# Strassen's seven products for two token chunks of a down-projection, with sums formed by accumulating DMAs

## The chip, the cores and the metric

One core of a Trainium2 chip runs one inference step of a one-layer hybrid decoder in float32. The metric is the device time of one execution in microseconds (us). The kernel uses TensorE (PE, matmuls; PEld its weight loads), VectorE (DVE), ScalarE (ACT), GpSimd (POOL) and SyncE (SP, which issues most DMAs).

## The reference, cut to what matters

The layer is an FFN, then attention and gated delta branches, then a second FFN (FFN 2). Only FFN 2 is touched.

```python
def swiglu(x, w_in, w_out):
    gate, up = jnp.split(x @ w_in, 2, axis=-1)
    return (jax.nn.silu(gate) * up) @ w_out
...
    y = h + 0.5 * rmsnorm(swiglu(rmsnorm(h, p['ffn2_pre']), p['ffn2_w_in'], p['ffn2_w_out']), p['ffn2_post'])
```

There are 1056 tokens (1024 of the prompt and 32 sampled), the model width is 1024, and D_FF is 2816, which is 22 tiles of 128. The down-projection is a 1056 x 2816 by 2816 x 1024 product.

## The kernel before

Each engine has its program written out by hand and waits on semaphores; nothing else orders the work. `ffn_units` builds both FFNs, `outputs_ffn` what surrounds FFN 2. Float32 products are made of two rounded halves: ScalarE casts a value to its high part, VectorE subtracts to get the low part, and TensorE does three matmuls (high by high, high by low, low by high).

*Gate stage.* Two of the 22 tiles of D_FF are computed plainly. For each of the other twenty (loop over t, line 2740) `product` does seven Strassen products of 24 matmuls with 264 columns. GpSimd makes four sums of the weight tiles in `s_buf` (lines 2829 to 2834), VectorE combines the products and multiplies gate by up in `pair_h`, and `store_h` writes the tile to `d_hid` in DRAM, in two halves of the tokens. SP loads the pair of weight tiles two ahead (`load_pair`).

*Down-projection.* Tokens are in three chunks: 384, 384 and 288 (`SPANS`). The loop over h goes through six passes: h // 2 is the chunk, h % 2 the half of 512 output columns. A pass has 22 steps k, one for each tile of D_FF, and each step has 4 output blocks x 3 matmuls (`out_step`, line 2897). A pass sums in four PSUM banks, the next one in the other four. The weight tile of step u is loaded by `load_unit` into one of eight 256 KB slots, cast by `unit_high` (2568) and split by `unit_low` (2572), three steps before TensorE uses it, into one of four slots. So a cast waits until TensorE has finished with the step four before it. The hidden tiles come back from `d_hid` through four staging buffers (`load_hid`), are cast (2594) and split (2600) into `hid_hi` and `hid_lo`, and serve both halves. The first ten are prepared within the last tile of the gate stage:

```python
    EARLY = {2: range(0, 3), 3: range(3, 6), 4: range(6, 8), 5: range(8, 10)}
```

*After a chunk.* `square` (ScalarE) and `copy_out` (VectorE) empty PSUM into `acc`; `sum_pool` (GpSimd, 2981), `sum_y` (PE, 2989) and `root_y` (ScalarE, 3001 and 3003, each with a table load) give the norm; `norm` (3010) and `resid` (3981) on VectorE scale and add the residual, which `res_load` brings; then TensorE transposes (`turn`, 4120) and ScalarE copies rows out (3849). These are placed into steps of the next passes by functions named `during(h, k)` for each engine. `turn_residual` (4141) and `res_row` (3853) do the same for the residual of chunk 2, whose own norm is applied at the very end.

## Time and profile before

| what | value |
|---|---|
| time, median of 3 runs | 3401.08 us (3397.26 to 3401.41) |
| span of the profiled execution | 3400.1 us |
| TensorE busy | 3305.8 us, 97% |
| VectorE, ScalarE, GpSimd busy | 1871.2, 1456.3, 700.0 us |
| DMA | 390.03 MB, mean 115 GB/s |

The profiled execution has no time of its own beside these; its span runs from its first to its last instruction. Busy times of matmuls overlap, because they are pipelined, so the rate of TensorE is read from starts or from long pieces, not from the mean duration.

### The profile page before, as it was taken

Reading aid. Unit: us, or ns where it says so; the run is one execution under the profiler, and the core shown is the slowest. Engines: PE = TensorE matmul, PEld = TensorE weight load, DVE = VectorE, ACT = ScalarE, POOL = GpSimd, SP = SyncE. Lnnn points to the kernel's source line nnn. Section 1 sums busy time; section 2 is a strip of 40 time slices with the busy share of each in tenths; the row PEclk is TensorE's granted clock in tenths of the full one; section 3 lists DMA queues with packets and bytes.
Section 4 is the critical chain, followed back from the end, with each engine's and each line's share of the span. In section 5 each row is a group of like instructions: output and inputs, shape, how many; then the busy total and the mean of one; then the engine's idle time right before and its main releaser. Section 6 shows DMA issues by size and latency. Waiting matters only on the chain. (4 is left out here: it accounts for less than half of the span.)

```text
span 3400.1 us, 70872 instructions
## 1 busy us (share of the span) xinstructions
PE 3305.8 (97%) x28190; PEld 3137.6 (92%) x28190; DVE 1871.2 (55%) x3334; ACT 1456.3 (43%) x3056; POOL 700.0 (21%) x651
## 2 busy tenths in 40 slices
PE   7999999998999999999999999999999899999999
PEld 7999999997888888877899999998999899999998
DVE  6655565764555555554455555554441855556555
ACT  5222234555555455443344444444323722223444
POOL 3323310112222222100022222222001332221000
PEclk9999999999999999999999999999999999999999
DMA  4222237742222222379511122224532322224664
GB/s 167 76 79 79 87 109 230 221 135 81 70 70 70 71 70 70 109 254 369 188 47 56 58 59 59 59 59 136 165 88 70 123 86 76 76 76 151 200 207 132
DMA packets 353606, 390.03 MB, mean 115 GB/s; under 512 B 22792, under 2 KB 259416, under 8 KB 353134
## 3 DMA queue, kind: packets, MB, share of 16 engines
q1 hardware_dynamic: 343126, 352.18, 33.1%
q0 software_dynamic: 10080, 33.05, 2.7%
q8 instruction: 228, 3.74, 0.5%
q14 instruction: 88, 0.72, 0.1%
q10 hardware_dynamic: 84, 0.35, 0.0%
HBM read 309.92 MB, written 75.57 MB: 113 GB/s over the span
## 5 line engine op out<-in xcount | busy, mean ns | idle before, releaser
L673 PE MATMUL ps<-p_hi,w_hi 128*128 128x352 f32 x912 | 305.6, 335 | 1.8 <-PEq L123 1.4
L673 PE MATMUL ps<-p_hi,w_lo 128*128 128x352 f32 x912 | 294.5, 323 | 0.0
L673 PE MATMUL ps<-p_lo,w_hi 128*128 128x352 f32 x912 | 294.0, 322 | 0.0
L2062 PE MATMUL ps<-p_hi,w_hi 128*128 128x352 f32 x840 | 291.0, 346 | 2.7 <-PEq L123 1.4
L2062 PE MATMUL ps<-p_hi,w_lo 128*128 128x352 f32 x840 | 277.2, 330 | 0.0
L2062 PE MATMUL ps<-p_lo,w_hi 128*128 128x352 f32 x840 | 277.2, 330 | 0.0
L673 PEld LDWEIGHTS ps<-p_hi,w_hi 128*128 128x128 f32 x912 | 173.1, 190 | 4.2 <-issue 2.7
L2897 PE MATMUL ps<-op_hid_hi,w_hi 128*128 128x384 f32 (+1 forms) x528 | 171.5, 325 | 3.7 <-DVE w_lo L2572 2.0
L673 PEld LDWEIGHTS ps<-p_lo,w_hi 128*128 128x128 f32 x912 | 173.2, 190 | 0.0
L2897 PE MATMUL ps<-f_hid_hi,w_hi 128*128 128x352 f32 x528 | 171.5, 325 | 1.6 <-DVE w_lo L2572 1.6
L673 PEld LDWEIGHTS ps<-p_hi,w_lo 128*128 128x128 f32 x912 | 172.2, 189 | 0.0
L2897 PE MATMUL ps<-f_hid_lo,w_hi 128*128 128x352 f32 x528 | 170.0, 322 | 0.0
L2897 PE MATMUL ps<-f_hid_hi,w_lo 128*128 128x352 f32 x528 | 169.9, 322 | 0.0
L2897 PE MATMUL ps<-op_hid_hi,w_lo 128*128 128x384 f32 (+1 forms) x528 | 169.6, 321 | 0.0
L2897 PE MATMUL ps<-op_hid_lo,w_hi 128*128 128x384 f32 (+1 forms) x528 | 169.6, 321 | 0.0
L2062 PEld LDWEIGHTS ps<-p_hi,w_hi 128*128 128x128 f32 x840 | 160.5, 191 | 8.2 <-issue 3.1
L2062 PEld LDWEIGHTS ps<-p_lo,w_hi 128*128 128x128 f32 x840 | 160.9, 192 | 0.2
L2062 PEld LDWEIGHTS ps<-p_hi,w_lo 128*128 128x128 f32 x840 | 160.5, 191 | 0.0
L2572 DVE TENSOR_TENSOR w_lo<-w_raw,w_hi 128x512 fp32r<-128x512 f32 x136 | 100.5, 746 | 83.2 <-ACT w_hi L2568 82.8
L414 ACT ACTIVATE at_prob<-ps,at_nmax 128x256 f32<-128x256 f32 (+7 forms) x128 | 94.2, 737 | 82.4 <-DVE at_nmax L520 80.7
L2568 ACT CAST w_hi<-w_raw 128x512 fp32r<-128x512 f32 x136 | 83.8, 620 | 100.5 <-PE ps L2897 100.1
L347 ACT ACTIVATE at_rotx<-ps 32x352 f32<-32x352 f32 x192 | 87.4, 455 | 88.6 <-DVE at_cosx L468 54.7
(707 smaller groups left out, 10374.4 us busy)
## 6 DMA issues: line engine op xcount, KB each, us to landing
w_raw<-in_ffn_w_out_dram SPq DMA_DIRECT2D x136, 256.0 KB, 3.4
w_raw<-in_w_in_dram SPq DMA_DIRECT2D x67, 512.0 KB, 4.2
sa_v<-in_cache_v_dram SPq DMA_DIRECT2D x120, 256.0 KB, 6.7
w_raw<-in_ffn_w_in_dram SPq DMA_DIRECT2D x48, 512.0 KB, 5.1
sa_k<-in_cache_k_dram SPq DMA_DIRECT2D x72, 256.0 KB, 5.5
f_s<-in_ffn_w_out_dram SPq DMA_DIRECT2D x64, 256.0 KB, 3.5
pair_s<-in_ffn_w_out_dram SPq DMA_DIRECT2D x64, 256.0 KB, 3.2
d_hid<-f_gb SPq DMA_DIRECT2D x44, 264.0 KB, 2.1
```

The lines of the kernel that those rows point to most:

```text
L347: ins = nc.scalar.mul(dst, src, HD ** -0.5 if kind == "q" else 1.0)
L414: nc.scalar.activation(pr[:, i % 2, a, 0:(i + 1) * P], m.ps[:, 2 + 2 * a:4 + 2 * a, :].rearrange("p b k -> p (b k)")[:, 0:(i + 1) * P], AC ...
L673: mm = nc.tensor.matmul(m.ps[:, bank, 0:CH], a[:, k, w], b[:, f, cols(c)], start=(f == 0 and i == 0), stop=(f == KT - 1 and i == 2))
L2062: mm = nc.tensor.matmul(m.ps[:, (k + c) % 2, 0:CH], a[:, k, f * P:(f + 1) * P], x[:, f, cols(c)], start=(j == 0), stop=(j == len(terms) - 1))
L2568: nc.scalar.copy(unit_slot(u, False), unit_raw(u)).then_inc(e.out_hi, 1)
L2572: nc.vector.tensor_tensor(unit_slot(u, True), unit_raw(u), unit_slot(u, False).bitcast(F32), ALU.subtract).then_inc(e.out_lo, 1)
L2897: mm = nc.tensor.matmul(m.ps[:, bank, 0:hi - lo], unit_slot(u, low_part)[:, o * P:(o + 1) * P], y[:, k, 0:hi - lo], start=(k == 0 and n == ...
```

## The change

Chunks 0 and 1 (768 tokens) are multiplied by Strassen's scheme. The 22 tiles of D_FF are split into two times 11 (KH), the output columns into two halves, the tokens into the two chunks. Seven products p of 11 steps each take the place of four passes of 22 steps. Chunk 2 keeps its two passes, now h = 7 and 8.

- *Weights.* Product 0 and 5 use a block of `w_out` as it is. The sums for products 1, 2 and 3 (33 tiles) are formed in DRAM during the gate stage: SP copies one tile to `d_w` (`copy_pairs`), GpSimd issues a DMA that adds the other (`add_pairs`). Products 4 and 6 load two tiles for each step and VectorE subtracts them (`w_sum`), 22 times.
- *Hidden tiles.* Tiles 11 to 21 are stored negated (`pair_h`), so that sums become differences. SP writes the first chunk of tiles 0 to 10 twice more (`store_sums`), and GpSimd's accumulating DMAs form the operands of products 0, 4, 5 and 6 in DRAM (`add_stored`, `add_lower`). VectorE forms that of product 3 (`x_sum`). Each operand is cast and split in three groups of 4, 4 and 3 tiles (`x_high`, `x_low`), each a single instruction.
- *Results.* A product's four banks are read in two pieces of 2 x 384. ScalarE writes blocks of `acc` first (`read_act`), VectorE adds to or subtracts from them (`read_dve`). `acc` now holds both chunks.
- *Order.* The work after chunk 0 goes into products 5 and 6, with the transposes of its rows at steps 7 to 9 of product 6; the work after chunk 1 goes into h = 7. The norm of chunk 1 is at step 9 of h = 7, where it had been at step 6 of h = 4; residual rows are still at steps 8, 10, 12. The cast of chunk 2's hidden tiles runs from product 6 into h = 7, and GpSimd makes their low parts (`rest_low`), in between its sums of squares.

```diff
+    KH = FT // 2
+    W3 = 3 * P
+    WL = T - 2 * W3
+    GROUPS = ((0, 4), (4, 8), (8, KH))
+    SOURCES = (((1, 1),), None, None, None, ((1, 0), (1, 1)), ((0, 0),), ((0, 1), (0, 0)))
...
+    COPIES = [(p, k) for p in PAIRED for k in range(KH)]
+    READ_ACT = (4, 6, 8, 8, 8, 8, 8)
...
+    def copy_pairs(sp, t):
+        for p, k in COPIES[2 * (t - 2):2 * (t - 1)]:
+            a, half = PAIRED[p][0]
+            sp.dma_start(d_w[p - 1, k], wout[:, k + KH * a, half * 512:half * 512 + 512]).then_inc(e.w_copied[t % 2], 16)
+    def add_pairs(pool, t):
+        if 2 * (t - 2) < len(COPIES):
+            pool.wait_ge(e.w_copied[t % 2], 16 * (2 * ((t - 2) // 2) + len(COPIES[2 * (t - 2):2 * (t - 1)])))
+        for p, k in COPIES[2 * (t - 2):2 * (t - 1)]:
+            a, half = PAIRED[p][1]
+            pool.dma_start(d_w[p - 1, k], wout[:, k + KH * a, half * 512:half * 512 + 512], accum_op=ALU.add).then_inc(e.w_added, 16)
...
+    def store_sums(sp, t):
+        for d in (d_first, d_sum):
+            sp.dma_start(d[t], hid[:, 0:W3]).then_inc(e.x_out, 16)
+    def add_stored(pool, s):
+        j = s - KH
+        if s < KH:
+            for a in range(2):
+                pool.wait_ge(e.h_out[a], 16 * (s + 1))
+            pool.wait_ge(e.x_out, 32 * (s + 1))
+            wait(pool, e.added[6], 16 * s)
+            pool.dma_start(d_sum[s], hid_part(s, 1), accum_op=ALU.add).then_inc(e.added[6], 16)
+            return
+        pool.wait_ge(e.h_out[0], 16 * (s + 1))
+        if j == 0:
+            pool.wait_ge(e.x_out, 32 * KH)
+            pool.wait_ge(e.added[6], 16 * KH)
+        wait(pool, e.added[0], 16 * j)
+        pool.dma_start(d_first[j], hid_part(s, 0), accum_op=ALU.add).then_inc(e.added[0], 16)
+        pool.wait_ge(e.h_out[1], 16 * (s + 1))
+        pool.dma_start(hid_part(j, 1), hid_part(s, 1), accum_op=ALU.add).then_inc(e.added[5], 16)
+    def add_lower(pool, s):
+        pool.wait_ge(e.added[0], 16 * (s - KH + 1))
+        pool.dma_start(hid_part(s, 0), hid_part(s, 1), accum_op=ALU.add).then_inc(e.added[4], 16)
+    def load_first_parts(sp, g):
+        lo, hi = GROUPS[g]
+        if g < 2:
+            sp.wait_ge(e.up_mm, 12 + N1 - 6)
+        else:
+            sp.wait_ge(e.up_mm, 12 + N1)
+        sp.wait_ge(e.added[0], 16 * hi)
+        sp.dma_start(FIRST[g], d_first[lo:hi].rearrange("k p n -> p k n")).then_inc(e.first_in[g], 16)
+    def load_quad(sp, p, k):
...
+        src = {1: (k, 0), 2: (KH + k, 1), 4: (KH + k, 0), 5: (k, 1)}
+        sp.dma_start(HOME[p][:, k, :], d_sum[k] if p == 6 else hid_part(*src[p])).then_inc(e.quad_in[p], 16)
...
+    def x_high(act, p, g):
...
+            act.wait_ge(e.up_mm, 12 + N1 - 7 + (2, 3, 4, 6)[(GROUPS[g][1] * W3 - 1) // (HALF * HT)])
+        elif p >= 2:
+            act.wait_ge(e.out_mm, KH * (p - 1))
+        nc.scalar.copy(x_slot(hid_hi, p, g), x_value(p, g)).then_inc(e.hid_hi, 1)
...
+    def w_sum(dve, v):
+        r = RAW_OF[v]
+        raw_there(dve, r)
+        raw_there(dve, r + 1)
+        nc.vector.tensor_tensor(unit_raw(r), unit_raw(r), unit_raw(r + 1), ALU.subtract).then_inc(e.w_sum, 1)
...
+    def w_high(act, v):
+        if v in SUM_OF:
+            act.wait_ge(e.w_sum, SUM_OF[v])
+        else:
+            raw_there(act, RAW_OF[v])
...
+            act.wait_ge(e.up_mm, 12 + N1 - 10 + v + 1)
...
+        if lower_rest(v):
+            nc.scalar.mul(unit_slot(v, False), unit_raw(RAW_OF[v]), -1.0).then_inc(e.out_hi, 1)
+        else:
+            nc.scalar.copy(unit_slot(v, False), unit_raw(RAW_OF[v])).then_inc(e.out_hi, 1)
...
+    def rest_high(act, n):
+        act.wait_ge(e.hid_full[n % 4], 16 * (n // 4 + 1))
+        act.wait_ge(e.out_mm, KH * 6 if n < 14 else KH * 7)
+        nc.scalar.copy(rest_tile(hid_hi, n), staged(2, n % 4)[:, 0:WL]).then_inc(e.rest_hi, 1)
+    def rest_low(pool, n):
+        pool.wait_ge(e.rest_hi, n + 1)
+        nc.gpsimd.tensor_tensor(rest_tile(hid_lo, n), staged(2, n % 4)[:, 0:WL], rest_tile(hid_hi, n).bitcast(F32), ALU.subtract).then_inc(e.rest_lo, 1)
...
+    def read_act(act, q):
+        if q in (0, 1, 2):
+            act.wait_ge(e.out_mm, KH * (q + 1))
...
+            for i in (1, 0):
+                for half in range(2):
+                    nc.scalar.mul(block_of(i, 0, half), pass_bank(q, half), -1.0).then_inc(e.read_act, 1)
...
+            for half in range(2):
+                nc.scalar.mul(block_of(1, 1, half), pass_bank(q, half), -1.0).then_inc(e.read_act, 1)
+        elif q == 2:
...
+    def add_block(q, i, j, sign=1.0):
+        for half in range(2):
+            y = block_of(i, j, half)
+            if q in (1, 2):
+                nc.vector.wait_ge(e.read_act, READ_ACT[q - 1] + half + 1)
+            if sign > 0:
+                nc.vector.tensor_tensor(y, pass_bank(q, half), y, ALU.add).then_inc(e.read_dve, 1)
+            else:
+                nc.vector.scalar_tensor_tensor(out=y, in0=pass_bank(q, half), scalar=-1.0, in1=y, op0=ALU.mult, op1=ALU.add).then_inc(e.read_dve, 1)
+    def read_dve(dve, q, second):
+        if not second:
+            dve.wait_ge(e.out_mm, KH * (q + 1))
+            wait(dve, e.read_dve, READ_DVE[q - 1])
+        if q == 1:
+            if not second:
+                add_block(q, 1, 0)
+        elif q == 2:
+            if not second:
+                add_block(q, 0, 0)
+        elif q == 3:
+            add_block(q, *((1, 1) if second else (0, 0)))
+        elif q == 4:
+            if not second:
+                add_block(q, 0, 0, -1.0)
+        elif q == 5:
+            add_block(q, *((1, 1) if second else (0, 1)))
+        elif not second:
+            add_block(q, 1, 1)
...
+            copy_pairs(sp, t)
+            store_h(sp, t, 0)
+            if t < KH:
+                store_sums(sp, t)
+            store_h(sp, t, 1)
+        for g in range(2):
+            load_first_parts(sp, g)
+        for r in range(4, 8):
+            load_raw(sp, r)
+        store_h(sp, FT - 1, 0)
+        store_h(sp, FT - 1, 1)
+        r = 8
+        def raws(v):
...
+        for v in range(NQ):
+            p, k = divmod(v, KH)
+            raws(v + 6 if p else v + 8)
+            if v == 0:
+                for n in range(4):
+                    load_quad(sp, 1, n)
+            elif v == 1:
+                for n in range(4, 8):
+                    load_quad(sp, 1, n)
+            elif v == 2:
+                for n in range(8, KH):
+                    load_quad(sp, 1, n)
+            elif v == 3:
+                load_first_parts(sp, 2)
+            elif 5 <= v <= 15:
+                load_quad(sp, 2, v - 5)
+            elif 22 <= v <= 32:
+                load_quad(sp, 4, v - 22)
+            elif 33 <= v <= 43:
+                load_quad(sp, 5, v - 33)
+            elif 44 <= v <= 54:
+                load_quad(sp, 6, v - 44)
+            elif v == 62:
+                for n in range(4):
+                    load_rest(sp, n)
+            elif p == 6 and k >= 3:
+                load_rest(sp, k + 1)
+            during(p, k)
+        for h in range(2):
+            for k in range(FT):
+                raws(NQ + h * FT + k + 6)
+                if h == 0 and 12 + k < FT:
+                    load_rest(sp, 12 + k)
+                during(7 + h, k)
+    def quad_scalar(act, during):
+        for v in range(NQ):
+            p, k = divmod(v, KH)
+            w_high(act, v + 3)
+            if p == 0:
+                if k == 5:
+                    x_high(act, 0, 2)
+                elif k in (7, 9):
+                    x_high(act, 1, (k - 7) // 2)
+            else:
+                if k == 0:
+                    read_act(act, p - 1)
+                elif p == 1 and k in (2, 5, 7, 9):
+                    x_high(act, 1 if k == 2 else 2, {2: 2, 5: 0, 7: 1, 9: 2}[k])
+                elif k in (2, 4, 6) and 1 < p < 6:
+                    x_high(act, p + 1, k // 2 - 1)
+                elif p == 6 and k >= 2:
+                    rest_high(act, k - 2)
+            during(p, k)
+        for h in range(2):
+            for k in range(FT):
+                v = NQ + h * FT + k
+                if v + 3 < NQ + 2 * FT:
+                    w_high(act, v + 3)
+                if h == 0 and 9 + k < FT:
+                    rest_high(act, 9 + k)
...
+    def quad_vector(dve, during):
+        for v in range(NQ):
+            p, k = divmod(v, KH)
+            w_low(dve, v + 3)
+            if v + 4 in SUM_OF:
+                w_sum(dve, v + 4)
+            if p == 0:
+                if k == 6:
+                    x_low(dve, 0, 2)
+                elif k in (8, 10):
+                    x_low(dve, 1, k // 2 - 4)
+            elif p == 1:
+                if k in (3, 6, 8, 10):
+                    x_low(dve, 1 if k == 3 else 2, {3: 2, 6: 0, 8: 1, 10: 2}[k])
+            else:
+                if k == 0:
+                    read_dve(dve, p - 1, False)
+                elif k == 1 and p == 2:
+                    x_sum(dve, 0)
+                elif k == 2:
+                    if p == 2:
+                        x_sum(dve, 1)
+                    read_dve(dve, p - 1, True)
+                elif k in (3, 5, 7) and p < 6:
+                    x_low(dve, p + 1, (k - 3) // 2)
+                elif k == 4 and p == 2:
+                    x_sum(dve, 2)
+            during(p, k)
+        for h in range(2):
+            for k in range(FT):
+                v = NQ + h * FT + k
...
+    def quad_gpsimd(pool, during):
+        for n in range(8):
+            rest_low(pool, n)
+        sum_pool(pool, 1, 1, 4)
+        for n in range(8, 11):
+            rest_low(pool, n)
+        sum_pool(pool, 1, 4, 6)
+        for n in range(11, 13):
+            rest_low(pool, n)
+        sum_pool(pool, 1, 6, 8)
+        for n in range(13, FT):
+            rest_low(pool, n)
+    def quad_tensor(pe, during, bank_free):
+        for p in range(7):
+            for k in range(KH):
+                v = KH * p + k
+                during(p, k)
+                pe.wait_ge(e.out_lo, v + 1)
+                for g in range(3):
+                    if k == GROUPS[g][0]:
+                        pe.wait_ge(e.hid_lo, part_count(p, g))
...
+                    for n, (low_part, y) in enumerate(((False, hid_hi), (False, hid_lo), (True, hid_hi))):
+                        mm = nc.tensor.matmul(m.ps[:, 4 * (p % 2) + o, 0:W3], unit_slot(v, low_part)[:, o * P:(o + 1) * P], y[:, x, :],
+                                              start=(k == 0 and n == 0), stop=(k == KH - 1 and n == 2))
+                mm.then_inc(e.out_mm, 1)
...
         dve.wait_ge(e.up_done, 6 + 2 * (t - 2) + 2 - a)
-        nc.vector.tensor_tensor(hid[:, halves(a)], hid[:, halves(a)], silu[:, halves(a)], ALU.mult).then_inc(e.h_done, 1)
+        if not quads or t < KH:
+            nc.vector.tensor_tensor(hid[:, halves(a)], hid[:, halves(a)], silu[:, halves(a)], ALU.mult).then_inc(e.h_done, 1)
+            return
+        nc.vector.scalar_tensor_tensor(out=hid[:, halves(a)], in0=hid[:, halves(a)], scalar=-1.0, in1=silu[:, halves(a)],
+                                       op0=ALU.mult, op1=ALU.mult).then_inc(e.h_done, 1)
 
     def vector(dve, scale_in, between, during):
...
+            if quads:
+                if t > 2:
+                    add_pairs(pool, t - 1)
+                if t > 2 + KH:
+                    add_lower(pool, t - 3)
+                add_stored(pool, t - 2)
+        if quads:
+            add_lower(pool, FT - 3)
+            add_stored(pool, FT - 2)
+            add_lower(pool, FT - 2)
+            add_stored(pool, FT - 1)
+            add_lower(pool, FT - 1)
+            during()
+            quad_gpsimd(pool, during)
 
...
+                nc.scalar.copy(row_of(6 + t).rearrange("p (b f) -> p b f", b=2), m.ps[:, 2:4, :]).then_inc(res_moved, 1)
 
             def during(h, k):
-                if h == 4 and k in (8, 10, 12):
+                if h == 3 and k in (7, 8, 9, 10):
+                    e.square(act, k - 7)
+                elif h == 5 and k in (1, 2):
+                    e.square(act, 2 + 2 * k)
+                    e.square(act, 3 + 2 * k)
+                elif h == 5 and k == 7:
+                    e.root_y(act, 0, 3)
+                elif h == 6 and k in (5, 6):
+                    e.square(act, 2 * k - 2)
+                    e.square(act, 2 * k - 1)
+                elif h == 6 and k in (7, 8, 9):
+                    row(k - 7)
+                elif h == 7 and k in (1, 2):
+                    e.square(act, 10 + 2 * k)
+                    e.square(act, 11 + 2 * k)
+                elif h == 7 and k in (8, 10, 12):
                     res_row((k - 8) // 2)
-                if h in (2, 4):
...
-                c = h // 2 - 1
-                if h in (2, 4):
-                    if 8 <= k < 12:
-                        e.norm(dve, c, 2 * (k - 8), 5 * KT)
-                        e.norm(dve, c, 2 * (k - 8) + 1, 5 * KT)
-                    elif k in (12, 13):
-                        resid(c, k - 12)
+                pairs = {(5, 9): (0, 0), (5, 10): (0, 1), (6, 1): (0, 2), (6, 3): (0, 3), (7, 10): (1, 0), (7, 11): (1, 1), (7, 12): (1, 2), (7, 13): (1, 3)}
+                sums_of = {(6, 4): (0, 0), (6, 5): (0, 1), (7, 14): (1, 0), (7, 15): (1, 1)}
+                if (h, k) in pairs:
...
 
             def during(h, k):
-                if h == 4 and k in (7, 9, 11):
+                if h == 5 and k == 6:
+                    pe.wait_ge(e.read_dve, e.READ_DVE[4])
+                    e.sum_y(pe, 0, 3)
+                if h == 6 and k in (7, 8, 9):
+                    turn(k - 7)
+                if h == 7 and k in (7, 9, 11):
                     turn_residual((k - 7) // 2)
-                if h == 4 and k == 17:
-                    pe.wait_ge(res_moved, 3)
-                if h == 5 and k == 10:
-                    pe.wait_ge(e.y_copied, 2 * KT + HALF)
+                if h == 7 and k == 8:
+                    e.sum_y(pe, 1, 0)
+                if h == 7 and k in (17, 18, 20):
+                    turn({17: 3, 18: 4, 20: 5}[k])
```

## Rows read from the trace of the kernel before

**Rows 1.** The page: span, busy times, the granted clock in 40 slices.
```profile
span 3400.1 us, 70872 instructions
...
PE 3305.8 (97%) x28190; PEld 3137.6 (92%) x28190; DVE 1871.2 (55%) x3334; ACT 1456.3 (43%) x3056; POOL 700.0 (21%) x651
...
PEclk9999999999999999999999999999999999999999
```

**Rows 2.** The chain that ended last, from 2700 us: start, length, what.
```profile
2709.02 392.84 PE ps L2887 x3216
...
3127.28 95.97 PE ps L2897 x552
...
3330.82 9.48 PE ps L2897 x72
```

**Rows 3.** Who waited for whom, 3113 to 3401: us in total, times, longest.
```profile
PE ps L2897 <- DVE w_lo L2572: 2.0, 2, 1.7
...
PE ps L2897 <- ACT plain L3849: 1.7, 2, 1.0
...
PE ps L4141 <- ACT plain L3853: 0.8, 1, 0.8
```

**Rows 4.** Windows: busy us by engine (instructions), clock, DMA share, GB/s.
```profile
core 0: us, PE busy (x) PEld busy (x) DVE busy (x) ACT busy (x) POOL busy (x), PEclk, DMA share, GB/s
2900.00:3000.00 100.00, 100.00 (x825) 100.00 (x824) 57.12 (x89) 27.26 (x48) 31.25 (x20) 1.00 0.28 81
3180.00:3190.00 10.00, 10.00 (x60) 10.00 (x59) 5.82 (x10) 4.93 (x10) 0.00 (x0) 1.00 1.03 361
3190.00:3200.00 10.00, 10.00 (x59) 10.00 (x58) 5.74 (x11) 5.17 (x10) 0.00 (x0) 1.00 0.85 252
```

**Rows 5.** A group of the gate stage: VectorE reading PSUM; busy, mean ns, idle.
```profile
L2774 DVE TENSOR_TENSOR op_gb<-ps,pair_tmp 128x528 f32<-128x528 f32 x19 | 13.4, 707 | 28.2 <-PE ps L2887 28.2
```

**Rows 6.** Groups of GpSimd, 500 to 1600 us: DMAs that it issues.
```profile
L615 POOL DMA_DIRECT2D d_gates<-at_gate x15 | 8.3, 556 | 28.5 <-ACT at_gate L358 28.5
L600 POOL DMA_DIRECT2D out_k_prompt_dram<-at_k_rows x8 | 7.9, 992 | 289.2 <-ACT at_k_rows L375 245.2 <-issue 44.0
```

**Rows 7.** DMA issues (KB, us to landing), and SP's waits, gate stage.
```profile
d_hid<-op_gb SPq DMA_DIRECT2D x38, 264.0 KB, 2.2
...
pair_s<-in_ffn_w_out_dram SPq DMA_DIRECT2D x64, 256.0 KB, 3.2
...
SPq L2510 <- DVE op_gb L2723: 331.8, 36, 14.8
```

**Rows 8.** The start of the down-projection: VectorE's timeline; TensorE's line 2897.
```profile
3125.91 0.71 DVE L2723 TENSOR_TENSOR op_gb<-op_gb 128x528 f32<-128x528 f32 x1 [0.71 <-ACT op_gb L2673]
3126.54 0.68 DVE L2572 TENSOR_TENSOR w_lo<-w_raw,w_hi 128x512 fp32r<-128x512 f32 x1
...
L2897 PE MATMUL ps<-op_hid_hi,w_hi x528: 289/334/631, 3119.1 to 3388.8; 128*128 128x384 f32 x118, 128*128 128x288 f32 x58
```

**Rows 9.** Groups of instructions by shape, 3113 to 3401 us.
```profile
L2572 DVE TENSOR_TENSOR w_lo<-w_raw,w_hi 128x512 fp32r<-128x512 f32 x68 | 49.1, 728 | 49.8 <-ACT w_hi L2568 49.4
...
L2568 ACT CAST w_hi<-w_raw 128x512 fp32r<-128x512 f32 x68 | 42.0, 621 | 58.8 <-PE ps L2897 58.6
...
L2600 DVE TENSOR_TENSOR op_hid_lo<-plain,op_hid_hi 128x384 fp32r<-128x384 f32 x44 | 24.9, 572 | 9.7 <-ACT op_hid_hi L2594 9.5
...
L2981 POOL TENSOR_TENSOR op_gb<-op_gb 128x384 f32<-128x384 f32 x14 | 16.4, 1171 | 210.1 <-ACT op_gb L2966 208.7
...
L2594 ACT CAST op_hid_hi<-plain 128x288 fp32r<-128x288 f32 x22 | 9.5, 431 | 5.2 <-DMA plain<-d_hid 5.1
L3010 DVE SCALAR_TENSOR_TENSOR acc_chunk<-acc_chunk,gain,op_gb 128x384 f32<-128x384 f32 x16 | 9.1, 612 | 0.0
...
L3981 DVE TENSOR_TENSOR acc_chunk<-acc_chunk,plain 128x1536 f32<-128x1536 f32 x4 | 7.0, 1752 | 0.0
...
L3853 ACT COPY plain<-ps 128x1024 f32<-128x1024 f32 x3 | 3.0, 1006 | 0.0
...
L3001 ACT ACT_TABLE_LOAD x2 | 2.6, 1283 | 0.0
```

373 lines of the change are left out of this document (307 added, 66 removed).

## The prediction

> **What bounds the kernel now.** I read the page first: TensorE is busy 3305.8 us of a span of 3400.1 us and its clock reads 9 in all forty slices [rows 1]. Next the chain that ended last, in order of time, for the stage that the change touches [rows 2]. From 2709.02 it is TensorE in one unbroken piece, the gate stage (3216 of its 3360 matmuls), and then the down-projection, again TensorE in long pieces. A kernel whose chain is one engine gets faster only by less work on it, or by fewer waits of it. The table of waits [rows 3] says how few there are in the down-projection: 2.0 us for VectorE's low parts and 1.7 us for ScalarE's row copies on PE's own rows, 0.8 for the residual transposes. So removed matmuls are worth their full price, and each microsecond by which another engine comes late is paid in full. The windows [rows 4] give the cover: while TensorE is full, VectorE is busy 57 of 100 us in the gate stage and 5.8 of 10 later, ScalarE 27 of 100 and 5 of 10. The DMA share is 0.28 in the gate stage, but 0.85 to 1.03 while hidden tiles and residual are loaded.
>
> **What is removed.** For token chunks 0 and 1 the product was 4 passes x 22 steps x 12 matmuls of 384 columns = 1056. Seven products x 11 steps x 12 are 924, so 132 go. Durations in the table overlap, so the price is the pitch: 552 matmuls in 95.97 us [rows 2] = 0.1739 us. That is -22.95 us. A step of 12 is 2.09 us, a product 23.0 us. Chunk 2 keeps its 528 matmuls of 288 columns (9.48 us for 72, 0.132 each; a step of 1.58 us). Transposes and sums on TensorE stay the same in number.
>
> **Gate stage.** Its matmuls don't change. One pair of tiles takes 168 matmuls x 392.84/3216 = 20.5 us. GpSimd is busy 31.25 of 100 us with its four sums [rows 4], 6.4 us of a pair, so 14.1 are free. It now issues accumulating DMAs in each pair: two weight sums and one hidden sum at first (pairs 3 to 12), five in pairs 14 to 18, four in 13 and 19. No accumulating DMA is in the trace. GpSimd's plain ones take 0.54 us (528 KB) to 0.99 us (512 KB) of its time [rows 6]: 2.7 to 5.0 us for five, hidden. Their waits are for stores that land 2.2 us after issue [rows 7] and were issued before GpSimd starts that pair, so nothing queues behind them for long; what is queued is the next pair's sums, which VectorE and ScalarE need about three products (9 us) before TensorE would starve. SP gains four plain DMAs in a pair (two 256 KB copies, two 192 KB); it waits 331.8 us of this stage for hidden tiles [rows 7], so their issue is covered. In bytes a pair has 1.5 MB at share 0.28; the change adds 0.9 MB of plain and up to 1.1 MB of accumulating transfers, each of which reads twice. Even at three times a plain one's price that is share 0.7. VectorE's 528-wide multiply gets a sign in 22 cases, beside idle time. I cost the stage at nothing; floor 0, ceiling under the rivals.
>
> **Start of the down-projection.** Before, VectorE's last gate product and the low part of step 3 come at 3125.9 to 3127.2 [rows 8], and TensorE, which begins at 3119.1, loses 1.7 us. After, ten hidden casts (5.5 us of VectorE, ten of 0.57) become two 1536-wide ones before step 3 (1.75 each, from the residual sum's row in [rows 9]), so VectorE is 2 us earlier and that wait goes. A new one comes at step 8: the third group of the first operand needs, from the last hidden half at about 3122, a store (2.2 us), an accumulate (I take 4 us: plain 256 KB ones land in 3.2), a load behind 2.2 MB of product 1's tiles and four weight tiles (3.2 MB at 361 GB/s, 9 us from 3124), its own 0.6 MB and a cast (1.2) and a low part (1.4). It is ready near 3139; step 8 is due at 3119.1 + 16.7 = 3135.8. +3.2, minus the 1.7: **+1.5 us** (0 to 7).
>
> **The seven products, VectorE.** Weights for step v+3 may be cast when step v-1 is done: 0.62 + 0.73 us, against 3 steps of 6.26, so VectorE may lag by 4.9 us before TensorE waits. Its operations, by [rows 9] where no other group is named: low part 0.73; weight sum 0.73; a 768-wide addition from PSUM 0.95 (0.707 for 528 in [rows 5], and 1.0 ns for each further element, the slope between the 512 and 1536 wide rows); low part of four tiles 1.75, of three 1.36; norm 0.61. Product 4: 11 low parts, 7 sums, 4 additions, 3 low parts of the next operand, 8.0 + 5.1 + 3.8 + 4.9 = 21.8 of 23.0 us, but front-loaded: steps 0 to 6 hold 17 us against 14.6. The lag, about 3, stays under 4.9. Products 1, 2, 3 and 5 hold less. Product 6: steps 0 to 5 hold 6 low parts, 6 sums, 4 additions, 4 norms and 2 residual sums = 4.4 + 4.4 + 3.8 + 2.4 + 3.5 = 18.5 us, after a start late by 1.7 (two norm pairs in product 5's last steps). At step 7, 14.6 us in, TensorE must transpose what the residual sums gave, ready at 20.2. **+5.4 us**, less 0.6 for the same wait of before. No row shows a queue as full as this, so 0 (transposes just in time) to 8.
>
> **DMA.** In product 4, and again in 6, a step needs two 256 KB weight tiles and one hidden tile of 192 KB (147 KB in 6): 721 kB in 2.09 us, 345 GB/s, against 220 before. [Rows 4] show 361 GB/s at share 1.03 and, ten microseconds later, 252 at 0.85, which is 296 at full share. By 361 nothing is lost; by 296 a step lasts 2.44 us, so 3.9 in each product, and the last residual's 1.18 MB in product 6 is 4.0 more: 11.8. The row nearest to this mix of tiles is the first, so **+1 us**. The Trainium skill (DMA: Bandwidth & Descriptors, Specifications) puts the HBM limit per core at about 358 GB/s; by that this term is 0 and the sum 1 us lower, and the 361 of the trace agrees.
>
> **Chunk 2's first half.** The norm of chunk 1 moves from step 6 to step 9, to between two residual-row copies. From step 8 ScalarE has a weight cast, a hidden cast (0.43) and a copy (1.0): 2.05; then step 9's casts and the root (two table loads of 1.28 and two passes of some 0.55), 1.05 + 3.7; then step 10's 2.05: 8.85 us. TensorE needs that second copy at step 11, 4.7 + 1.2 us in: 2.9 late. The norms and residual sums then end near 20.7, TensorE's step 17 comes at 19.1: 1.6. Together 4.5, against 1.8 in [rows 3]: **+2.7 us** (0 to 5). GpSimd's 22 low parts (0.9 each, three quarters of the 384-wide row) and seven sums of 1.17 [rows 9] are 28 us, over some 54: hidden.
>
> **Sum.** -22.95 + 1.5 + 5.4 - 0.6 + 1 + 2.7 = -12.95. The shown times are 3401.08 median (3397.26 to 3401.41); the profiled execution's span is 3400.1, so what lies around it is about 1.0 us and stays. 3401.1 - 13.0 = **3388 us**.
>
> **The rivals.**
> All new work is hidden: VectorE's rows are long enough and every wait above is an overestimate. Then only the matmuls count and the old 2.3 us go too: 3376. For it: 5 to 6 us of lag come from adding mean durations. Against: product 6's queue is full by count. 0.16.
> DMA binds products 4 and 6, and queued weight tiles arrive late: 296 GB/s instead of 361, and the accumulated lag cannot be won back, up to +11.8 - 1: 3395 to 3399. For it: the second window of [rows 4]. 0.22.
> GpSimd sets the pace of the gate stage, the case that ends slower. It decides from 14.1/5 = 2.8 us for an accumulating DMA. At 4 us each, a pair with five takes 6.4 + 20 = 26.4 instead of 20.5, five times, and one with four 22.4, twice: +33, so 3421. Against it: 0.54 to 0.99 in [rows 6]; for it: none of those computes. The Trainium skill (SBUF — State Buffer, Who interferes with whom) says that software descriptor generation is starved while VectorE is in a two-port mode, and that its tensor_tensor has none. By that rule this case stays away; no row here has a DMA of GpSimd's beside such a mode, so the trace doesn't settle it. The chance is 0.12.
> The forecast as summed, 3383 to 3393: 0.50.
>
> **How the numbers follow.** 0.2% (6.8 us) is about what a measurement of this kernel can tell from no change. Faster: the forecast's 0.50 less 0.02, the hidden case's 0.16, and a little of the DMA case, 0.03: 0.67. Same: most of the DMA case and the edge of the forecast: 0.21. Slower: 0.12. The range goes from 3375 (all hidden) to 3402 (both 296 GB/s and the upper ends of the start); it leaves out the GpSimd case and slivers.
>
> **What the changed profile would show.** 924 matmuls of 384 columns at a pitch of 0.174; the gate stage still one piece of 3216 or more at 0.122; GpSimd's accumulating DMAs under 1 us each in it, with its four sums starting every 20.5 us. One wait of TensorE for a low part of hidden tiles some 17 us into the down-projection; one of about 5 us at the transposes in product 6, whose releaser is VectorE's residual sum; two in chunk 2's first half, released by ScalarE's residual copy and VectorE's residual sum. DMA share near 1 in products 4 and 6. The prediction is wrong if the gate stage stretches, if weights arrive late in products 4 and 6 (VectorE's weight sums waiting for DMA), or if VectorE's reads of PSUM take much more than 0.95 us.

## The result: no gain, and 28 us of waits and half clock where 10 us of waits were forecast

The changed kernel took 3406.7 us in the median of 20 runs (3399.55 to 3413.99), the kernel before 3400.23 us beside it (20 runs, 3394.21 to 3405.44): ratio 1.0018, 95% interval 1.0012 to 1.0025. Forecast was 3388 (3375 to 3402). So it is slower by 0.18%, 6 us, and 19 us off the forecast.

The profiled execution is the longest of its 20 runs (3413.99 us). The page of the changed kernel, beside [rows 1]: 132 matmuls fewer, and nearly as much busy TensorE.
```profile
span 3412.4 us, 70726 instructions
...
PE 3297.4 (97%) x28058; PEld 3127.3 (92%) x28058; DVE 1892.9 (55%) x3303; ACT 1464.0 (43%) x3030; POOL 784.2 (23%) x750
...
PEclk9999999999999999999999999899999999999999
...
q0 software_dynamic: 21168, 50.35, 6.1%
```
The one 8 in the clock's row is slice 26 (2133 to 2218 us), in a stage that the change doesn't touch; slices of 85 us are too coarse for what follows. The chain that ended last (start, length, what), beside [rows 2]:
```profile
2714.32 410.27 PE ps L3408 x3360
...
3150.49 69.22 PE ps L3054 x384
```
The gate stage is one piece of 3360 matmuls, 0.1221 us each, the same pitch as before. It starts 5.3 us later than in [rows 2]: that much of the difference of the two traces was there before any touched line. From here on I compare the rest of the span, from the first matmul of the down-projection: 3400.1 - 3119.1 = 281.0 us before, 3412.4 - 3124.4 = 288.0 after, +7.0. This comparison leaves the jitter of earlier stages out and agrees with the 6 us of the medians. It is still one execution of each kernel. The part behind the last matmul of chunk 2 is 10.7 us before and 11.9 in the changed kernel, but 10.9 to 11.0 in ten of the twelve edited kernels below, none of which touches it: about 1 us of the 7.0 is chance of this execution, and "rest" makes each edit below look some 1 us better than it is.

Who waited for whom on TensorE from 3120 on (total, times, longest), beside [rows 3]:
```profile
PE ps L3054 <- DVE op_hid_lo L2761: 9.2, 1, 9.2
PE ps L4677 <- DVE acc_chunk L4537: 8.0, 2, 6.6
PE ps L4700 <- ACT plain L4397: 5.1, 2, 4.7
PE ps L3061 <- ACT plain L4393: 1.0, 1, 1.0
PE ps L3061 <- DVE w_lo L2798: 0.7, 1, 0.7
PE ps L3054 <- DVE w_lo L2798: 0.6, 2, 0.4
PE ps L3061 <- DVE w_lo L2795: 0.3, 1, 0.3
```
That is 24.9 us against 4.5. Three waits make 20.5 of it: at step 8 of product 0 (L3054), at chunk 0's transposes in product 6 (6.6 of L4677) and at a residual row block in chunk 2's first half (4.7 of L4700). The windows of these places, beside [rows 4], and of the gate stage (busy us by engine, clock, DMA share, GB/s):
```profile
2720.00:3120.00 400.00, 400.00 (x3293) 400.00 (x3292) 230.68 (x355) 111.94 (x195) 180.56 (x149) 1.00 0.64 154
3140.00:3160.00 20.00, 10.78 (x49) 10.49 (x48) 7.49 (x8) 7.24 (x10) 0.00 (x0) 0.74 0.88 300
3280.00:3300.00 20.00, 13.44 (x72) 13.12 (x71) 18.88 (x24) 8.55 (x18) 6.89 (x6) 0.81 0.79 257
3320.00:3340.00 20.00, 14.17 (x89) 13.21 (x89) 6.54 (x10) 13.00 (x22) 8.20 (x10) 0.83 0.93 319
```
The last column but two, the granted clock, is what I had no term for. It is 1.00 in the gate stage and 0.74 to 0.83 in the three windows with a long wait; of the other windows of 20 us up to 3380 only the one behind 3300 is below 1.00 (0.94). TensorE's timeline behind the first (start, length) shows what that means for work:
```profile
3150.49 0.66 PE L3054 MATMUL ps<-op_hid_hi,w_hi 128*128 128x384 f32 x1 [9.22 <-DVE op_hid_lo L2761]
3150.94 0.52 PE L3054 MATMUL ps<-op_hid_lo,w_hi 128*128 128x384 f32 x1
3151.26 0.52 PE L3054 MATMUL ps<-op_hid_hi,w_lo 128*128 128x384 f32 x1
...
3155.74 0.34 PE L3054 MATMUL ps<-op_hid_lo,w_hi 128*128 128x384 f32 x1
3155.91 0.34 PE L3054 MATMUL ps<-op_hid_hi,w_lo 128*128 128x384 f32 x1
```
Starts are 0.32 us apart until 3155.74 and 0.17 after it: the clock stood at its lower level of 1.2 GHz. These 5.25 us hold 16 matmuls, worth 2.8 us at 0.1739: 2.5 us lost. The length of this stretch is in part chance: behind the same wait (8.9 to 9.7 us) it is 2.8 us in e3, 3.0 in e7 and 5.5 in e10, so 1.4 to 2.8 us are lost. In product 6 the eight transposes and the step behind the 6.6 us wait take 5.6 us (3296.74 to 3302.34), where the next transposes take 0.9 and a step 2.1: 2.6 lost. Behind the 4.7 us wait the clock is low until 3336.6, 4.5 us, of which half is lost: 2.2.

The sheet of the changed part: -22.95 (matmuls), +20.4 (waits, 24.9 - 4.5), +7.3 (half clock) = +4.8, of the +7.0 seen; 1.2 of the missing 2.2 us lie behind chunk 2's last matmul (10.7 us there before, 11.9 after).

### The profile page after: what moved, and what is told of

The parts are those of the page before. It is cut to its first block and busy times, and to the rows that moved or that the text cites. A ratio compares the mean times of both kernels' runs of the same rounds, so it can differ in the third digit from the quotient of the medians.

```text
span 3412.4 us, 70726 instructions
## 1 busy us (share of the span) xinstructions
PE 3297.4 (97%) x28058; PEld 3127.3 (92%) x28058; DVE 1892.9 (55%) x3303; ACT 1464.0 (43%) x3030; POOL 784.2 (23%) x750
## 5 line engine op out<-in xcount | busy, mean ns | idle before, releaser
L3054 PE MATMUL ps<-op_hid_hi,w_hi 128*128 128x384 f32 x308 | 105.7, 343 | 9.8 <-DVE op_hid_lo L2761 9.2
L517 DVE TENSOR_TENSOR ps<-ps,cst 128x128 f32<-128x128 f32 x128 | 37.5, 293 | 135.5 <-PE ps L740 132.2
L3408 PE MATMUL ps<-p_hi,w_hi 128*128 128x264 f32 x384 | 109.6, 285 | 1.8 <-DVE w_lo L2540 1.8
L3408 PE MATMUL ps<-p_hi,w_lo 128*128 128x264 f32 x384 | 109.9, 286 | 0.0
L3408 PE MATMUL ps<-p_lo,w_hi 128*128 128x264 f32 x384 | 109.8, 286 | 0.0
```

The costliest lines, as they stand in the source:

```text
L517: nc.vector.tensor_tensor(s[:, i * P:(i + 1) * P], s[:, i * P:(i + 1) * P], m.cst[:, C_CAUS:C_CAUS + P], ALU.add).then_inc(masked, 1)
L3054: mm = nc.tensor.matmul(m.ps[:, 4 * (p % 2) + o, 0:W3], unit_slot(v, low_part)[:, o * P:(o + 1) * P], y[:, x, :], start=(k == 0 and n == 0 ...
L3408: mm = nc.tensor.matmul(m.ps[:, bank + n, 0:HB], w_slot(s, lo)[:, w], y, start=(i < 4 and f == 0 and q == 0), stop=((i >= 4 or i == 1) and ...
```

## What makes the three waits

**Step 8.** SP's timeline (start, length, what it issues) from the last hidden half on, cut:
```profile
3125.98 3.23 SPq L2519 DMA_DIRECT2D d_hid<-op_gb  x2
...
3129.74 2.05 SPq L2732 DMA_DIRECT2D plain<-d_hid  x4
...
3136.81 0.57 SPq L2656 DMA_DIRECT2D w_raw<-d_w_sums  x1
3137.48 1.13 SPq L2715 DMA_DIRECT2D plain<-d_first  x1
```
The store goes out at 3125.98, GpSimd's accumulating DMA at 3128.30, and it lands 4.7 us later, at 3133. The load of the third group (L2715) goes out only at 3137.48, since eleven operand tiles and four weight tiles stand ahead of it in SP's order. These fifteen issues keep SP at work without a pause from 3129.26 to 3137.38, 0.54 us each. The load then lands 9.2 us after its issue, at 3146.66: the DMA share is 0.92 from 3129 to 3137.5 (273 GB/s) and 1.08 from there to 3146.7 (339 GB/s). The cast, a weight tile's low part and its own low part take until 3150.34. The loads that SP issues from 3129.26 to 3133.29 land after 4.5 to 5.1 us, the next ones, up to this one, after 7.0 to 9.2. Between them, at 3133.52 and 3134.05, GpSimd issues its last two accumulating DMAs, whose sums are for products 4 and 5, the first of which begins at 3227.85. Whether they make the loads slower is not shown, since no run moved them.

**Product 6.** VectorE is busy 18.9 of 20 us; the two residual sums of chunk 0 (L4537) run from 3291.47 and 3294.93, while step 7 was due at 3290.2.

**Chunk 2's first half.** ScalarE's timeline:
```profile
3321.88 0.62 ACT L2790 CAST w_hi<-w_raw 128x512 fp32r<-128x512 f32 x1 [4.12 <-DMA w_raw<-in_ffn_w_out_dram]
...
3332.89 1.28 ACT L3538 ACT_TABLE_LOAD   x1
3334.18 0.58 ACT L3538 ACTIVATE op_gb<-ps,cst 128x384 f32<-128x384 f32 x1
3334.78 1.28 ACT L3540 ACT_TABLE_LOAD   x1
```
I had put ScalarE's root between two row copies and only that. But ScalarE had already waited 4.12 us for a weight tile, and 1.3 us for three of the next four: chunk 1's residual (1.5 MB) and three row stores (0.5 MB each) had been issued from 3312.37 to 3320.32, ahead of those tiles.

## The experiments

Theory: these three waits, each with the half clock behind it, give the gain back; the DMAs of the gate stage cost nothing. Rivals: DMA traffic as such, or a VectorE that is short of time everywhere. Each kernel is the changed one with an edit; "changed" stands at 1.0018 of the kernel before, and "rest" is the rest of the span as above (288.0 us for it, 281.0 before).

### e1: the third group's load earlier
```diff
             elif v == 1:
+                load_first_parts(sp, 2)
+            elif v == 2:
                 for n in range(4, 8):
...
-            elif v == 3:
-                load_first_parts(sp, 2)
```
(The last operand tiles of product 1 go to step 3.)

> Theory (three waits of the down-projection, each followed by matmuls at half clock, give the 23 us back): SyncE now issues the load of the third operand group at step 1, as soon as the last summing DMA has landed, in place of after eleven operand loads. The load is issued near 3133 instead of 3137.5 and has less ahead of it, so step 8 of product 0 waits 1 to 3 us instead of 9.2, and the 2.4 us of half clock behind it go too: 7 to 11 us faster than the changed kernel, ratio to the kernel before 0.9985 to 0.9995 in place of 1.0018. Rival (the DMA queues are simply full in product 0): the load lands no earlier, or product 1's operands come late by the same amount and the wait moves to the start of product 1: within 2 us of the changed kernel.

3395.6 us, ratio 0.9989 (0.9979 to 0.9999), rest 279.1. The wait is 2.9 us:
```profile
3117.82 1.99 SPq L2732 DMA_DIRECT2D plain<-d_hid  x4
3119.86 0.43 SPq L2662 DMA_DIRECT2D w_raw<-in_ffn_w_out_dram  x1
3121.10 0.37 SPq L2715 DMA_DIRECT2D plain<-d_first  x1
```
```profile
PE ps L4677 <- DVE acc_chunk L4537: 8.0, 2, 6.6
PE ps L4700 <- ACT plain L4397: 5.0, 2, 4.8
PE ps L3054 <- DVE op_hid_lo L2761: 2.9, 1, 2.9
```
The load goes out 8.6 us after the first matmul, not 13.1, and lands 7.4 us later, and the other two waits stand where they were. By the medians it is about 10 us faster; in the trace the seven products are 7.1 us shorter (6.3 of wait, the rest half clock), all from where one load stands in a queue. Product 1 isn't late, so the rival falls. But the DMA share is 1.06 from 3120 to 3140 (357 GB/s), so the 2.9 us that are left may well be the DMA's.

### e2: chunk 0's transposes later
```diff
-            return (6, 4, 6, 2, 0, 2)[i]
+            return (6, 4, 0, 2, 0, 2)[i]
...
-                if h == 6 and k in (7, 8, 9):
-                    turn(k - 7)
+                if h == 6 and k in (9, 10):
+                    turn(k - 9)
+                if h == 7 and k == 4:
+                    turn(2)
```
(ScalarE's copies, the bank waits and the third row's store follow.)

> Transposes of chunk 0's first two row blocks at steps 9 and 10 of product 6, the third at step 4 of chunk 2's first half. Theory: VectorE ends its residual sums of chunk 0 at 3296.6 whatever TensorE does, and step 9 is due at 3294.2, so the wait of 6.6 us falls to 0 to 2.5 and the half clock behind it (2.6 us) goes: 6 to 9 us faster than the changed kernel, ratio to before 0.999 to 1.0. Rival (VectorE is the bound from product 5 on, the weight sums with it): the wait only moves, to the weight tiles of steps 9 and 10 or to the first read of chunk 2: less than 2 us gained.

3400.1 us, ratio 1.0002 (0.9993 to 1.0011), rest 281.7 (-6.3). Nothing of the 6.6 us wait is left at chunk 0's transposes, and the clock from 3280 to 3300 is 1.00. But weight tiles now come late:
```profile
PE ps L3054 <- DVE w_lo L2798: 2.8, 4, 1.7
PE ps L3061 <- DVE w_lo L2798: 1.4, 1, 1.4
```
Of the first row 0.6 us in two waits are product 4's, as in the changed kernel; 0.5 and 1.7 us are new, in product 6. The second was 0.7. By the ratios the gain is 5.4 us, just under the 6 to 9 of the theory, by the trace 6.3: the theory holds in the main, and some of the rival with it.

### e3: the big transfers out of chunk 2's first steps
```diff
-                elif h == 7 and k == 0:
+                elif h == 6 and k == 9:
                     res_load(1)
-                elif h == 7 and k in (2, 3, 4):
-                    store_row(k - 2)
+                elif h == 7 and k in (10, 12, 14):
+                    store_row((k - 10) // 2)
```


> Chunk 1's residual load (1.5 MB) goes out at step 9 of product 6 and the three row stores (0.5 MB each) at steps 10, 12 and 14 of chunk 2's first half, in place of steps 0 to 4 of that half. Theory (the wait of 4.7 us before residual row block 1 is there because ScalarE got its weight tiles late behind these 3 MB, with the table loads on top): ScalarE is no longer late at step 7, the wait falls to 2 to 3 us, and most of the 2 us of half clock goes: 3 to 5 us faster than the changed kernel. Rival A (ScalarE's table loads alone make that wait): no more than 1 us gained. Rival B (1.5 MB more in product 6 holds up the two-tile loads there): a new wait in product 6, slower by 1 to 4 us.

3400.35 us, ratio 0.9997 (0.9988 to 1.0006), rest 282.6 (-5.4). By the ratios that is 7.1 us, more than expected; in the trace chunk 2 is 3.5 us shorter, the 3 to 5 expected, and the other 1.8 us are a shorter half clock in the products and the part behind the last matmul, which this edit doesn't touch. TensorE's waits at the row blocks (start of the matmuls behind them, length):
```profile
PE ps L4700 <- ACT plain L4397: 3.6, 2, 3.0
```
They were 5.1. ScalarE no longer waits for the DMA of a weight tile in steps 0 to 6; what is left is its root, 3.0 us late, against the 2.9 that the prediction had worked out for it. Rival B did not come.

### e4: no weight sums in the gate stage
Products 1 to 3 load the first tile of each pair, so the second is left out of the result; the 66 DMAs of `copy_pairs` and `add_pairs` are gone.

> The 33 copies and 33 accumulating DMAs of weight tiles in the gate stage are left out; products 1 to 3 read the first tile of each pair instead of the sum, so they compute something else with the same matmuls. Theory (the gate stage hides these DMAs, and they leave nothing behind that the down-projection waits for): within 1.5 us of the changed kernel, perhaps 1 us better since the last SwiGLU sum is issued somewhat earlier on GpSimd. Rival (17 MB of extra traffic and GpSimd's 33 issues of 0.96 us delay the store-and-sum chain that ends in the load of the third operand group): the wait of 9.2 us shrinks by 3 us or more and the kernel is 3 to 8 us faster.

3404.7 us, ratio 1.0009 (1.0000 to 1.0018), rest 287.0 (-1.0), wait at step 8 9.1 us, the gate stage the same 410.29 us for 3360 matmuls. The medians leave anything from 0 to some 8 us open; the trace shows 1.0 in the down-projection and nothing in the gate stage. The 66 DMAs are hidden.

### e5 and e8: all three edits, and the row blocks spread


> The edits of e1, e2 and e3 together. Theory (the three waits are separate places, so their gains add): 9.9 + 5.4 + 7.1 us off the changed kernel by the three ratios, 3384 us, ratio to before 0.9945 to 0.9965. Rival (one shortage behind all three, of DMA or of VectorE, so that a cleared place moves its wait to the next): not more than the best one alone gave, ratio 0.998 or above.

3390.85 us, ratio 0.9973 (0.9964 to 0.9982), rest 272.4. Against the changed kernel that is 0.45%, 15.3 us, of the 22.4 which the single gains add up to: between theory and rival. The shortfall of 7 us is, by the medians alone, within their noise, but the traces have it: without the part behind the last matmul the single edits gain 7.8, 5.4 and 4.3 us, 17.5 in sum, and the three together 14.5. The table of waits says where the 3 us went:
```profile
PE ps L3061 <- ACT plain L4393: 4.2, 2, 3.2
PE ps L4704 <- ACT plain L4397: 3.3, 2, 3.0
PE ps L3054 <- DVE op_hid_lo L2761: 2.9, 1, 2.9
```
Chunk 2's first matmul takes over the bank pair of row block 1, whose transposes e2 has moved to just ahead of it; it waits 3.2 us for it. The clock dips there too (0.80 from 3293 to 3299).

e8 adds, in chunk 2's first half:
```diff
-                if h == 7 and k in (7, 9, 11):
-                    turn_residual((k - 7) // 2)
+                if h == 7 and k in (7, 11, 14):
+                    turn_residual({7: 0, 11: 1, 14: 2}[k])
```
(ScalarE's copies follow at steps 8, 12 and 15.)

> e5 and the last two residual row blocks turned at steps 11 and 14 of chunk 2's first half (copied at 12 and 15), in place of 9 and 11 (10 and 12). Theory (what is left of the wait before row block 1 is ScalarE's root, 3.7 us between two row copies, and PSUM's bank pair is handed over by these copies): the 3.0 us wait left in e3's trace goes, 2 to 4 us faster than e5. Rival (ScalarE is short of time over the whole half, so the wait only moves to the weight tiles): within 1 us of e5.

3390.35 us, ratio 0.9968 (0.9958 to 0.9979), rest 275.2: by the runs no difference from e5 that can be told, by its trace 2.8 us longer. The 3.0 us wait is 0.4, and the one at chunk 1's transposes, 1.4 in e5, is 3.8. VectorE's residual sums of chunk 1 hang on the same root and end no earlier; TensorE merely arrives there sooner. The rival was right in the time, for another reason than it gave.

### e6: the wait filled with matmuls
```diff
+                        if p == 0 and g == 2:
+                            pe.wait_ge(e.up_sum, 2 * (FT - 2))
+                            pe.wait_ge(e.gate_sum, FT - 2)
+                            for n in range(44):
+                                nc.tensor.matmul(m.ps[:, 4, 0:W3], hid_hi[:, 0, 0:P], hid_hi[:, 0, :], start=True, stop=True)
                         pe.wait_ge(e.hid_lo, part_count(p, g))
```


> The changed kernel with 44 matmuls of 384 columns that nobody reads (7.7 us at the 0.174 us of full clock) put ahead of TensorE's wait for the third operand group. Theory (the granted clock falls because TensorE stood idle for 9.2 us, and the half clock behind it costs time): the wait left is 1 to 2 us, the following matmuls start 0.174 us apart and not 0.32, and the down-projection is 2 to 3 us shorter in the trace. Rival (the clock falls there for another reason, or the half clock costs nothing since the matmuls then wait for weight tiles anyway): the half clock stands in the same place or the length does not change.

3399.86 us, ratio 1.0004 (0.9995 to 1.0013), rest 284.0 (-4.0). The extra matmuls take 7.79 us and leave a wait of 1.40; the same 384 matmuls behind it, against 69.22 us:
```profile
3143.99 66.85 PE ps L3059 x384
```
```profile
3140.00:3160.00 20.00, 18.60 (x107) 18.28 (x107) 12.26 (x14) 13.58 (x18) 0.00 (x0) 1.00 0.80 260
```
2.4 us come back by doing 44 useless matmuls, the clock stays at 1.00, and the operand is as late as ever. That is the price of half clock by itself. The rest of the gain in the span (1.6 us) has no part in this edit; 1.0 of it is the part behind the last matmul.

### e7, e10 and e11: what fills VectorE in product 6
e7 cuts product 6's eleven weight sums to 64 of 512 columns and leaves the other 448 unsummed:
```diff
+        w = 64 if v >= KH * 6 else 512
...
```


> VectorE's eleven weight sums of product 6 cover 64 of 512 columns (the rest of those weights is left unsummed); all loads and waits stay. Theory (the transposes of chunk 0 wait 6.6 us because VectorE is full from product 5 on): some 0.5 us less in each of the eleven, of which seven to nine lie ahead of the last residual sum, so it ends 4 to 5 us earlier; the wait falls to 2 to 3 us, the half clock behind it goes: 4 to 7 us faster than the changed kernel. Rival (the tiles' loads, two per step, set VectorE's pace): the residual sums end at the same distance from the start of product 6 and the time stays within 1.5 us.

3400.5 us, ratio 1.0006 (0.9997 to 1.0015), rest 284.0, wait 5.0 us. A gain of 4 us, yet the wait fell by 1.6 us where 3.6 to 4.6 were expected. VectorE had the time and could not use it:
```profile
3276.73 0.22 DVE L2768 TENSOR_TENSOR w_raw<-w_raw,pair_s 128x64 f32<-128x64 f32 x1 [2.88 <-DMA pair_s<-in_ffn_w_out_dram]
3279.28 1.75 DVE L4538 TENSOR_TENSOR acc_chunk<-acc_chunk,plain 128x1536 f32<-128x1536 f32 x1
```
So loads are a second limit behind VectorE. e10 moves the 1.18 MB of the last residual from step 0 of product 6 to step 7, e11 does both.

> The changed kernel with the 1.18 MB load of the last residual at step 7 of product 6 in place of step 0. Open question: what holds VectorE in product 6, its own work or the loads of two weight tiles a step behind that transfer. Theory (its own work: in the changed kernel it idles 0.3 us in product 6): the wait before chunk 0's transposes stays at 6 to 7 us and the time within 1.5 us of the changed kernel. Rival (the loads): the wait falls below 4 us, 3 to 5 us faster.

3402.3 us, ratio 1.0008 (0.9999 to 1.0016), rest 283.7, wait 5.0: between theory and rival in the wait, and the intervals of this and the changed kernel overlap.

> e10 and e7 together: VectorE's weight sums of product 6 cut to 64 columns, the last residual's load moved to step 7. Theory (VectorE's work is the first limit and that load the second: in e7 VectorE waited 2.9 us for a weight tile behind it): the 2.9 us go, the wait before the transposes falls from e7's 5.0 to 1.5 to 2.5 us, 2 to 4 us faster than e7. Rival (something else delays the tile, so the idle time of VectorE stays): within 1 us of e7.

3398.2 us, ratio 0.9990 (0.9980 to 0.9999), rest 277.7, wait 0.8. That is 5 us better than e7, more than expected (the two intervals touch), and the wait falls by more than the edits gave apart, 5.8 us against 1.6 and 1.6: the residual sums start at 3281.74 and 3284.14, and step 7 is due at 3285.1. Of the 4.2 us from e7 to e11, 2.9 are the wait for the weight tile, which is gone; another 1.2 are two VectorE operations that GpSimd slows in e7 and not in e11 (last section). So VectorE's own work and the transfer ahead of its weight tiles both hold product 6.

### e9 and e12: two more arrangements
e9 is e8 with chunk 0's second and third row blocks in banks 0 and 1 at steps 4 and 6 of chunk 2's first half, and chunk 1's at steps 18 to 20.

> The edits of e8, with chunk 0's second and third row blocks turned at steps 4 and 6 of chunk 2's first half in banks 0 and 1, and chunk 1's row blocks turned at steps 18, 19 and 20 of it in place of 17, 18 and 20. Theory (in e5 and e8 one of the cleared waits came back at the next hand-over: 3.2 and 3.4 us at the first matmul of chunk 2's first half, which took over the bank pair of row block 1 before ScalarE had copied it, and 3.75 us before chunk 1's transposes): the first of the two goes with the half clock behind it (1.6 us), the second falls by the 1.5 us of a step: 4 to 7 us faster than e8, ratio to the kernel before 0.9950 to 0.9957. Rival (VectorE and ScalarE are behind there whatever the order of the row blocks): the wait moves once more, within 1.5 us of e8, ratio 0.9964 to 0.9972.

3390.1 us beside 3397.1, ratio 0.9980 (0.9969 to 0.9991), rest 272.2. That is above the range of theory and rival alike, though its interval reaches into the rival's; the mechanism is the rival's: the wait at the bank pair is gone, and 1.7 and 2.5 us for weight tiles, 1.2 for a row copy and 2.1 for the residual sums stand in the trace instead.

> e5 (all three moves) and the last residual's load at step 7 of product 6. Theory (VectorE is the first limit, DMA is not): within 1.5 us of e5, ratio to the kernel before 0.9968 to 0.9978. Rival (the crowded loads of product 6 hold e5 as well): 2 to 4 us faster than e5.

3394.6 us, ratio 0.9987 (0.9978 to 0.9996), rest 273.9: no gain over e5. The ratio is 0.0014 above e5's and outside the theory's range, with intervals that overlap; by the trace it is 1.5 us longer. The rival is refuted. ScalarE and VectorE now get their tiles for chunk 2 late (a new wait of 1.75 us at 3300).

e5, e8, e9 and e12 beat both kernels, by 0.13 to 0.32% against the kernel before; e1 alone does by 0.11%, with an interval that ends at 0.9999. e8's ratio is the best, and the runs can't tell it from e5's.

## Why the prediction was wrong, step by step

- **Matmuls, -22.95: right.** In e6 the 384 matmuls of the chain took 0.1741 us each.
- **Gate stage, 0: right, but partly by luck**, for its parts cost more than I took. GpSimd's groups there (busy, mean ns) show an accumulating DMA at 0.96 us for a weight tile and 1.17 to 1.73 for the 192 KB of a hidden tile, where I had 0.54 to 0.99; still under the 2.8 from which it would have decided. The DMA share is 0.64. I had said 0.7 even at three times a plain transfer's price, but that sum was wrong: (1.5 + 0.9 + 3 x 1.1) / 1.5 x 0.28 is 1.06. It fitted because the price was lower. The software queue, which carries the accumulating DMAs, took a share of 26.8% for 16.72 MB here and the hardware queue 35.4% for 46.02 MB, 2.1 times as much for a byte.
```profile
L2677 POOL DMA_DIRECT2D d_w_sums<-in_ffn_w_out_dram x33 | 27.3, 955 | 42.6 <-DMA d_w_sums<-in_ffn_w_out_dram 42.6
...
L2702 POOL DMA_DIRECT2D d_hid<-d_hid x10 | 17.3, 1728 | 4.4 <-DMA d_hid<-op_gb 4.4
```
- **Start of the down-projection, +1.5: the step that failed most.** Measured +7.5 for the waits (9.2 - 1.7) and +2.5 for the clock. The accumulate (4.7 landed, 4 taken) was right. What failed is the load's landing. I reckoned the load as bytes in a common pipe: 3.2 MB ahead of it, through at 13.9 us behind the first matmul, and then its own 0.6 MB alone, 1.6 us. It is issued at 13.1 us, about there, but lands 9.2 us later, at 22.2 us, where my terms give 15.5. DMA moved only 2.3 MB from 3129 to 3137.5 (273 GB/s, not 361) and 3.1 MB until the load landed, of which 0.6 are its own; and even the first of these loads, with little ahead of them, took 4.5 us to land. Since step 8 is 16.7 us behind the first matmul, a load issued at 13.1 could not be in time, and I took its place behind fifteen others as given. e1 shows it: issued 4.5 us earlier, it lands 6.3 us earlier, and the wait is 6.3 us shorter. (My terms add up to some 3137, not to the 3139 that I wrote, so the term as worked out was smaller still.)
- **Product 6, +5.4: right in place and releaser, low in size** (6.6, and 2.6 for the clock; 20.2 - 14.6 is 5.6, where I wrote 5.4). Durations were right: 947 ns for the addition from PSUM (0.95 taken), 1.81 us for four tiles' low part (1.75). Missed: ScalarE's root in product 5 (3268.0 to 3271.7), behind which VectorE is idle for 1.7 us at 3272, shortly before product 6 begins at 3275.45, and GpSimd's low parts (below).
- **DMA, +1, and the rival that DMA binds.** In product 4, at a DMA share of 0.86, there are only 0.6 us of waits: the rival did not happen as told. In product 6 (share 0.80) the loads do hold VectorE once its work is cut (e7, e11). Nor is 361 GB/s a ceiling in this case: the page of the kernel before has 369 GB/s in one of its slices of 85 us.
- **Chunk 2's first half, +2.7: half of the cause.** Waits there are 7.2 us (4.7, 0.7, 0.4, 1.4) against 0.8, and 2.2 for the clock. (I had subtracted 1.8; the 1.0 us of it at 3352.60 lies in chunk 2's second half and is still there, so my own waits gave +3.7.) The root's part was as predicted (3.0 us in e3, 2.9 worked out); the other is the queue of 3 MB ahead of the weight tiles. The change moves these transfers there from passes with steps of 2.09 us to a half with steps of 1.58 us and hidden tiles of its own, and I had priced DMA in products 4 and 6 alone. e3 shows it.
- **Half clock: no term at all**, 7.3 us over three places. With the waits as I had forecast them (3.2 and 5.4 us) there would probably have been some of it too: in e5 waits of 2.9 and 3.2 us are each followed by a dip, though one of 3.0 us is not.

Together: waits and half clock came to +27.7 us where I had +10.0, and the matmuls gave what I had said. What stays open: some 1 us of the sheet beside the 1.2 behind the last matmul, and how much of product 6's lateness is GpSimd's. Rows put 1.2 us on it (last section), but no run varied it alone.

## What to carry to other kernels

For each new operand, walk through its queue's order instruction by instruction: it is issued when the queue comes to it, not when it is ready, and each issue ahead of it costs time (here 0.54 us). It also shares the DMA engines with what is issued around it: here 9.2 us from issue to landing for 0.6 MB. Price a wait of the matmul engine at its length plus the half clock behind it, here 2.2 to 2.6 us for waits of 4.7 to 9.2. And do not add the gains of single repairs: three of 7.8, 5.4 and 4.3 us in the traces gave 14.5, because the next hand-over was never far behind.
